# Paired token scores, output projections by seven products, fewer identity products at the start and a first refill in halves, in a one-core attention and mixture-of-experts block

## The chip, the cores and the metric

The kernel runs on one core of one Trainium2 chip. The metric is the device time of one execution in microseconds (us), the median of the runs that were made. All data are float32. The engines are PE (TensorE), DVE (VectorE), ACT (ScalarE), POOL (GpSimd) and SP (SyncE, which issues most of the DMAs).

## What is computed

A block of one layer on 256 tokens of width 1024, with 256 memory rows: a token mixer, cross attention and a mixture of experts, each added to the running `x`. In the mixer, `nsa_mixer` scores each query against compressed keys, selected keys and window keys; with 256 tokens every block of keys is selected and the window holds all of them, so the two token softmaxes (selected, window) run over all earlier tokens. Cut to what the change touches:

```
s = einsum(q, k) * DA**-0.5            # 8 heads of 64, masked to kpos <= t; k_slc and k_win
p = softmax(s)                         # per head; then o = p @ v, gated
merged = sigmoid(gate_a) * (y_a @ w_up_a) + sigmoid(gate_b) * (y_b @ w_up_b)
x = x + merged @ w_o_mix               # 256 x 1024 by 1024 x 1024  ("om")
...
x = x + o @ w_o                        # the same shape, after cross attention  ("ro")
...
y = sum over the 4 best of 32 experts: ((u + 1) * g * sigmoid(1.702 g)) @ w_down[e]
```

## The kernel before

**Order of work.** Each engine has one hand-written stream of instructions, and semaphores join them. PSUM has eight banks of 128 x 512; every group of products has a name, and `group_order` lists the groups in the order in which PE makes them. `placed_groups` gives group i the bank i modulo 8. `begin(name)` makes PE wait until the bank's former group is drained, `end(name, ...)` counts it filled, and `drain` counts it drained. Engines that wait for a group call `filled_of` or `drained_of`.

**Stages.** First x is turned, normalized and projected (q, keys, values, gates). Then comes a loop of nine steps h over the eight heads. In step h PE turns the probabilities of head h-1 (`ta`, `tb`), makes the token scores of head h (`sc{h}_0`, `sc{h}_1`, L1103) and "filler" groups of 16 products (gates, keys and values of cross attention), besides pieces of the second mixer. DVE masks the scores (L1734) and takes maxima (L1738), ACT exponentiates (L737) and scales (L746). Heads 2c and 2c+1 lie in rows 0 to 63 and 64 to 127 of chunk c of `qT`.

**Output projections.** `project_and_turn` (PE) and `residual_and_turned` (DVE) run twice, for "om" and for "ro". PE makes four groups of eight products with 512 columns, one for each token tile t and each half n of the output; DVE adds each group to `x_tok` (L1833). Between them PE turns the sums into the feature layout (L875, L1215) and DVE applies the gain (L1569).

**Weights.** `ring` has six slots of 2 MB, which 22 pieces use in turn (`PIECES`); `LAST_USE` names the group whose filling frees a slot. The 32 experts follow: six pieces of 2 MB each, `gu0` to `gu3` and `dn0`, `dn1`. Even experts use the ring; odd ones have five slots of their own (`r_odd`) made from buffers of the earlier stages, and share the ring's slot of `dn1`. SP issues the pieces in a fixed order and waits before each until its slot is free. Pieces of experts 0 and 1 are loaded during the earlier stages (`first_block`, `odd_half`, `odd_piece`); `even_heads(1)` then waits for expert 0 to free `gu0` and starts the refills.

**Experts.** `expert_block` takes 64 slots of tokens: `gate_up` reads gu0 to gu3 (L1331), then the former block's result is scattered (L1324), hidden rows are turned, and `down` reads dn0 and dn1. `gather_half` (L1308) fetches tokens.

**Start.** `keep_busy(o, n)` (L905) makes n products of the identity with itself into a bank that nobody reads. Here it is called with 5, 4, 3 and 8. A float32 product is two MATMUL rows in the trace; a turn is one.

```
            for n, t in ((0, 0), (0, 1), (1, 0)):
                residual(prefix, n, t, scale)
```

## Time and profile before

| | |
|---|---|
| median of three runs | 1299.54 us (1298.63 to 1300.12) |
| the profiled execution, its own time | 1298.83 us |
| span of its profile | 1297.1 us |
| mean granted TensorE clock | 0.991 |
| PE busy | 1244.9 us, 96% |
| DVE, ACT, POOL busy | 288.7 us, 145.3 us, 8.2 us |
| DMA | 454.70 MB, mean 351 GB/s |

The profile is of one execution. An engine's busy share is a mean over stages with different limits, so it has to be read by stage. A wait is put down to the engine, the tile and the line that ended it. In the trace the duration of a MATMUL row contains its fill and drain; consecutive rows overlap, so the time of many is read from the start of the first and of what follows, or from the chain of waits, which doesn't count an overlap twice.

### The profile page before, as it was taken

To read this page: it belongs to the slowest core of one execution; us is meant where nothing else is said; L and a number is where in the kernel's file an instruction comes from. 1 tells how busy PE (TensorE), PEld (TensorE's weight loads), DVE (VectorE), ACT (ScalarE), POOL (GpSimd) and SP (SyncE) were. 2 spreads that over 40 slices of the span, in tenths; PEclk is the share of its full clock that TensorE was granted. 3 is DMA by queue.
4 is the path that set the end of the run, shared out by engine and by line. 5 is a ranking of instruction groups with operands and counts; after the bars stand their busy time and mean duration, and the time that the engine had idled before them with its cause. 6 is when DMAs were issued, how large, how long until landed. Compare 5 with 4: busy or idle time off the path is not lost.

```text
span 1297.1 us, 14906 instructions
## 1 busy us (share of the span) xinstructions
PE 1244.9 (96%) x6197; PEld 614.1 (47%) x6197; DVE 288.7 (22%) x697; ACT 145.3 (11%) x325; POOL 8.2 (1%) x34
## 2 busy tenths in 40 slices
PE   9999999999999999999999999999989899999986
PEld 8868886757644343333343333443333344333322
DVE  2362234321132221111121111221111132211112
ACT  2223232101310000000000000000000000000001
POOL 1000000000000000000000000000000000000000
PEclk9999999999999999999999999999999999999998
DMA  9953233357559999999999999999999999999995
GB/s 332 318 194 110 85 131 113 115 195 268 203 195 401 428 428 427 426 427 428 429 429 428 428 429 429 427 428 428 428 428 428 428 428 427 427 427 428 427 425 238
DMA packets 60451, 454.70 MB, mean 351 GB/s; under 512 B 7228, under 2 KB 14072, under 8 KB 35064
## 3 DMA queue, kind: packets, MB, share of 16 engines
q1 hardware_dynamic: 58168, 452.49, 84.9%
q10 hardware_dynamic: 2240, 1.58, 0.4%
q8 instruction: 34, 0.56, 0.2%
q14 instruction: 9, 0.07, 0.0%
HBM read 453.00 MB, written 1.05 MB: 350 GB/s over the span
## 4 chain that ended last, share of the span: by engine, by line
PE 68%; DMA 29%; SPq 1%; issue 1%; DVE 1%; ACT 0%; POOL 0%; DVEq 0%; POOLq 0%; ACTq 0%
PE ps L1331 30%; DMA r_odd<-in_w_gu_dram 17%; PE ps L886 13%; DMA ring<-in_w_down_dram 11%; PE ps L893 7%; PE ps L1308 3%; PE ps L1324 3%; PE ps L1405 2%; PE ps L939 1%; PE ps L1103 1%; PE ps L1432 1%; SPq L494 1%; PE ps L1427 1%; PE ps L905 1%; PE ps L1252 1%
## 5 line engine op out<-in xcount | busy, mean ns | idle before, releaser
L1331 PE MATMUL ps<-r_odd,r_memT 128*64 128x512 f32 x1024 | 226.7, 597 | 15.3 <-DMA r_odd<-in_w_gu_dram 15.2
L1331 PE MATMUL ps<-ring,r_memT 128*64 128x512 f32 x1024 | 225.8, 594 | 11.9 <-DMA ring<-in_w_gu_dram 11.2
L1331 PE MATMUL ps<-ring,r_kx 128*64 128x512 f32 x768 | 176.9, 609 | 11.2 <-DMA ring<-in_w_down_dram 11.2
L1997 DVE TENSOR_SCALAR r_ga<-ps 128x512 f32<-128x512 f32 x32 | 22.1, 692 | 637.6 <-PE ps L1331 637.6
L1331 PEld LDWEIGHTS ps<-r_odd,r_memT 128*64 128x64 f32 x1024 | 73.4, 138 | 166.4 <-issue 137.2
L1331 PEld LDWEIGHTS ps<-ring,r_memT 128*64 128x64 f32 x1024 | 71.8, 137 | 160.2 <-issue 135.7
L886 PE MATMUL ps<-r_odd,ring 128*128 128x256 f32 x576 | 129.5, 383 | 0.0
L886 PEld LDWEIGHTS ps<-r_odd,ring 128*128 128x128 f32 x576 | 109.5, 192 | 18.0 <-issue 3.2
L1331 PEld LDWEIGHTS ps<-ring,r_kx 128*64 128x64 f32 x768 | 54.9, 140 | 130.0 <-issue 108.0
L827 ACT ACTIVATE r_ga<-r_ga 128x512 f32<-128x512 f32 x32 | 20.2, 630 | 462.8 <-DVE r_ga L1997 462.8
L1308 PE MATMUL ps<-r_dm,r_x 128*128 128x128 f32 x512 | 65.8, 282 | 0.0
L1324 PE MATMUL ps<-r_kx,r_dm 64*128 64x512 f32 x256 | 63.6, 615 | 0.7 <-ACT r_kx L833 0.7
L1308 PEld LDWEIGHTS ps<-r_dm,r_x 128*128 128x128 f32 x512 | 62.8, 197 | 1.6 <-DVE r_dm L1927 0.8
L1331 PE MATMUL ps<-r_gbx,r_kx 128*64 128x512 f32 x256 | 58.5, 598 | 0.8 <-DVE r_kx L2010 0.8
L833 ACT ACTIVATE r_kx<-ps 128x512 f32<-128x512 f32 x32 | 19.1, 597 | 333.9 <-PE ps L1331 333.9
L893 PE MATMUL ps<-ring,r_memT 128*128 128x512 f32 x112 | 49.2, 595 | 0.0
L1324 PEld LDWEIGHTS ps<-r_kx,r_dm 64*128 64x128 f32 x256 | 22.0, 186 | 41.3 <-issue 39.7
L1935 DVE TENSOR_TENSOR r_memT<-ps,sm 128x512 f32<-128x512 f32 x32 | 22.1, 692 | 64.6 <-PE ps L1308 64.6
L1331 PEld LDWEIGHTS ps<-r_gbx,r_kx 128*64 128x64 f32 x256 | 16.9, 136 | 40.6 <-issue 27.4
L1405 PE MATMUL ps<-r_ga,r_kx 32*64 32x512 f32 x256 | 35.8, 612 | 0.0
L893 PEld LDWEIGHTS ps<-ring,r_memT 128*128 128x128 f32 x112 | 21.0, 190 | 25.5 <-issue 25.2
L886 PE MATMUL ps<-r_memT,ring 128*128 128x256 f32 x128 | 28.6, 381 | 0.0
(342 smaller groups left out, 804.1 us busy)
## 6 DMA issues: line engine op xcount, KB each, us to landing
ring<-in_w_gu_dram SPq DMA_DIRECT2D x64, 2048.0 KB, 27.9
r_odd<-in_w_gu_dram SPq DMA_DIRECT2D x60, 2048.0 KB, 27.5
ring<-in_w_down_dram SPq DMA_DIRECT2D x47, 2048.0 KB, 22.6
r_gbx<-in_w_down_dram SPq DMA_DIRECT2D x15, 2048.0 KB, 30.2
ring<-in_w_in_dram SPq DMA_DIRECT2D x7, 2048.0 KB, 13.7
r_odd<-in_w_gu_dram SPq DMA_DIRECT2D x8, 1024.0 KB, 13.3
ring<-in_w_k_x_dram SPq DMA_DIRECT2D x2, 2048.0 KB, 9.5
ring<-in_w_v_x_dram SPq DMA_DIRECT2D x2, 2048.0 KB, 7.9
```

Source lines behind the costliest of these rows:

```text
L494: sp.dma_start(odd_slot[j], gu_dram[e, j] if j < 4 else dn_dram[e, j - 4]).then_inc(odd_loaded[j], 16)
L827: nc.scalar.activation(sig, gact, ACT.Sigmoid, scale=1.702).then_inc(sig_done, 1)
L833: nc.scalar.activation(y_slot, ps[:, ZBK, :], ACT.Copy).then_inc(yslot_ready, 1)
L886: last = mm(o[:, j * T:(j + 1) * T], w(k), src[:, k, :], start=(k == 0), stop=(k == kk - 1))
L893: last = mm(o, src[:, k, t * P:(t + 1) * P], w[:, k, 0:n], start=(k == 0), stop=(k == C - 1))
L905: mm(o[:, 0:P], ident[:], ident[:], start=True, stop=True)
L1308: last = mm(ps[:, buf, c * P:(c + 1) * P], x_rows[:, t, 2 * q + c // 2, c % 2], place[:, t], start=(t == 0), stop=(t == 1))
L1324: last = mm(ps[:, YB + 2 * t + n, :], scat[half, t * P:(t + 1) * P], y_slot[half, :], start=False, stop=False, skip_group_check=True)
L1331: last = mm(ps[n * SLOTS:(n + 1) * SLOTS, bk, :], stationary_, moving(n), start=start, stop=stop, skip_group_check=True)
L1405: mm(ps[n * SLOTS:(n + 1) * SLOTS, GBK + b, :], cur[q * NE:(q + 1) * NE, :], bgu_rows[q * NE:(q + 1) * NE, :], start=True, stop=False, ski ...
L1935: V.tensor_tensor(xg[:, buf, 4 * q:4 * q + 4], ps[:, bank_, :].rearrange("p (c s) -> p c s", c=4), gain_half[q], ALU.mult).then_inc(xg_rea ...
L1997: V.tensor_scalar(gact, ps[:, GBK, :], 7.0, None, ALU.min).then_inc(g_limited, 1)
```

## The change

- **Token scores.** For even h both heads h and h+1 are made in step h, their products alternating between rows 0 to 63 and rows 64 to 127. The odd head's two groups have banks 6 and 7 to themselves in this stage; all other groups of the stage share banks 0 to 5.
- **Output projections.** Each is cut into 2 x 2 blocks and made by seven products of blocks (P1 to P7, each four PE products with 512 columns) in place of eight. DVE makes four sums of blocks of the source (512 elements a row, in `sums`, the buffer `r_tp`) and four sums of blocks of the weights (2048 elements a row, in place in the ring), and adds every product to one to four quarters of `x_tok`: 14 additions in place of 4.
- **First refill.** Expert 2's `gu0` is loaded in two halves, the first as soon as expert 0 has used that half.
- **Order on SP.** Since `sums` lies in the buffer of an odd slot, `odd_half(1, 1, 0)` goes behind P5 of "ro", and `dn0` of expert 0 ahead of it.
- **Start.** `keep_busy` is called with 2, 1, 2 and 6.

```diff
+SEVEN = (1, 2, 3, 6, 7, 5, 4)
+ADDED_TO = {1: ((0, 1), (0, 0), (1, 0), (1, 1)), 2: ((0, 1),), 3: ((0, 0),), 6: ((0, 0), (1, 0), (1, 1)),
+            7: ((1, 0), (1, 1)), 5: ((0, 0), (1, 0)), 4: ((1, 1),)}
...
-            g += [f"sc{h}_0", f"sc{h}_1"] + filler_names(h)[:1]
+            if h % 2 == 0:
+                g += [f"sc{h + m}_{t}" for t in range(TT) for m in range(2)]
+            g += filler_names(h)[:1]
...
-    g += ["om0_0", "om0_1", "om1_0", "tx0", "tx1", "om1_1", "tx2", "tx3"]
+    g += [f"omP{n}" for n in SEVEN] + ["tx0", "tx1", "tx2", "tx3"]
...
+    first, last = order.index("sc0_0"), order.index("ub0")
+    pairs, turn = [], 0
+    for i, name in enumerate(order):
+        if first <= i < last and name[:2] == "sc" and int(name[2]) % 2:
+            pairs.append((name, BANKS - 2 + int(name[4])))
+            continue
+        n = BANKS - 2 if first <= i < last else BANKS
+        pairs.append((name, turn % n))
+        turn += 1
...
+        sums = r_tp.rearrange("p (s k t) -> p s k t", s=4, k=4)
...
+            first_block(range(4, 5))
+            filled_of(sp, "roP5")
             odd_half(1, 1, 0)
-            first_block(range(4, 6))
+            first_block(range(5, 6))
             sp.wait_ge(sq_done, 7)
             odd_half(1, 2, 1)
             filled_of(sp, "rt")
             odd_half(1, 1, 1)
 
-            even_heads(1)
+            s = eslot["gu0"]
+            rows2 = ring[:, s].rearrange("p (k n) -> p k n", k=2)
+            sp.wait_ge(first_half_freed, 1)
+            sp.dma_start(rows2[:, 0], gu_dram[2, 0][:, 0]).then_inc(first_half_loaded, 16)
+            sp.wait_ge(freed[s], 1)
+            sp.dma_start(rows2[:, 1], gu_dram[2, 0][:, 1]).then_inc(loaded[s], 16)
+            even_heads(1, range(1, HEADS))
...
-                        drained_of(act, f"{prefix}0_{t}")
-                        drained_of(act, f"{prefix}1_{t}")
+                        drained_of(act, f"{prefix}P{(5, 4)[t]}")
...
-            keep_busy(bank("q1"), 5)
+            keep_busy(bank("q1"), 2)
...
-            keep_busy(bank("q1"), 4)
+            keep_busy(bank("q1"), 1)
...
-            keep_busy(bank("q1"), 3)
+            keep_busy(bank("q1"), 2)
...
-            keep_busy(bank("q1"), 8)
+            keep_busy(bank("q1"), 6)
...
-                    for t in range(TT):
-                        o = begin(f"sc{h}_{t}")
-                        n = P * (t + 1)
-                        for b in range(2):
-                            last = mm(o[:, b * n:(b + 1) * n], qT[half * DA:(half + 1) * DA, c, t * P:(t + 1) * P],
-                                      kskw[half * DA:(half + 1) * DA, b, g, 0:n], start=True, stop=True)
-                        end(f"sc{h}_{t}", last)
+                    if h % 2 == 0:
+                        c, g = h // 2, h // PAIRS
+                        for t in range(TT):
+                            n = P * (t + 1)
+                            oo = [begin(f"sc{h + m}_{t}") for m in range(2)]
+                            for b in range(2):
+                                for m in range(2):
+                                    strip = slice(m * DA, (m + 1) * DA)
+                                    last = mm(oo[m][:, b * n:(b + 1) * n], qT[strip, c, t * P:(t + 1) * P],
+                                              kskw[strip, b, g, 0:n], start=True, stop=True)
+                                    if b == 1:
+                                        end(f"sc{h + m}_{t}", last)
...
+            def project_and_turn(prefix, piece_name, src, turned, ready, turn):
+
+                w1, w2 = wslot(f"{piece_name}1", C, 512), wslot(f"{piece_name}0", C, 512)
+
+                def product(n, lhs, rhs, part=range(4)):
+                    o = begin(f"{prefix}P{n}") if part[0] == 0 else bank(f"{prefix}P{n}")
+                    for k in part:
+                        last = mm(o, lhs(k), rhs[:, k], start=(k == 0), stop=(k == 3), skip_group_check=True)
+                    if part[-1] == 3:
+                        end(f"{prefix}P{n}", last)
+
+                def upper_left(k):
+                    ready(k)
+                    return src[:, k, 0:P]
+
+                def upper_right(k):
+                    ready(4 + k)
+                    return src[:, 4 + k, 0:P]
+
+                weights(f"{piece_name}1")
+                product(1, upper_left, w1[:, 0:4])
+                product(2, upper_right, w1[:, 4:8])
+                weights(f"{piece_name}0")
+                pe.wait_ge(sums_ready, 5 * turn + 1)
+                product(3, lambda k: sums[:, 3, k], w2[:, 4:8])
+                pe.wait_ge(sums_ready, 5 * turn + 3)
+                product(6, lambda k: sums[:, 1, k], w1[:, 0:4])
+                product(7, lambda k: sums[:, 2, k], w2[:, 0:4])
+                pe.wait_ge(sums_ready, 5 * turn + 4)
+                product(5, lambda k: sums[:, 0, k], w2[:, 4:8])
+                pe.wait_ge(sums_ready, 5 * turn + 5)
+                product(4, lambda k: src[:, 4 + k, P:2 * P], w1[:, 4:8], range(2))
+                drained_of(pe, f"{prefix}P5")
                 transpose4(f"{turned}0", x_tok, 0)
                 transpose4(f"{turned}1", x_tok, 1)
-                token_group(prefix, piece_name, src, 1, 1, ready)
+                product(4, lambda k: src[:, 4 + k, P:2 * P], w1[:, 4:8], range(2, 4))
                 oo = [begin(f"{turned}2"), begin(f"{turned}3")]
                 for t in range(TT):
-                    drained_of(pe, f"{prefix}1_{t}")
+                    drained_of(pe, f"{prefix}P{(2, 4)[t]}")
...
+                    if is_block(i, 2) and j == 0:
+                        pe.wait_ge(first_half_loaded, 16)
...
+                        if is_block(i, 0) and kk == 0:
+                            last.then_inc(first_half_freed, 1)
...
+            def residual_and_turned(prefix, piece_name, src, scale, turned, g0, turn):
+
+                w1, w2 = wslot(f"{piece_name}1", C, 512), wslot(f"{piece_name}0", C, 512)
+                b11, b21, b12, b22 = w1[:, 0:4], w1[:, 4:8], w2[:, 0:4], w2[:, 4:8]
+                a11, a12, a21, a22 = (src[:, k:k + 4, t:t + P] for t in (0, P) for k in (0, 4))
+
+                def product_added(n):
+                    name = f"{prefix}P{n}"
+                    filled_of(dve, name)
+                    for t, half in ADDED_TO[n]:
+                        xv = x_tok[:, t, half * 512:(half + 1) * 512]
+                        last = V.scalar_tensor_tensor(out=xv, in0=bank(name), scalar=scale, in1=xv, op0=ALU.mult, op1=ALU.add)
+                    drain(name, last)
+                    drained_of(dve, name)
+
+                link(V.tensor_tensor(sums[:, 0], a21, a22, ALU.add))
+                V.tensor_tensor(sums[:, 2], a11, a21, ALU.subtract)
+                link(V.tensor_tensor(sums[:, 1], sums[:, 0], a11, ALU.subtract))
+                V.tensor_tensor(sums[:, 3], a12, sums[:, 1], ALU.subtract).then_inc(sums_ready, 1)
+                for slot in (f"{piece_name}0", f"{piece_name}1"):
+                    dve.wait_ge(loaded[slot_of[slot]], need[slot])
+                V.tensor_tensor(b12, b22, b12, ALU.subtract).then_inc(sums_ready, 1)
+                dve.wait_ge(sums_ready, 5 * turn + 2)
+                filled_of(dve, f"{prefix}P1")
+                V.tensor_tensor(b11, b12, b11, ALU.add).then_inc(sums_ready, 1)
+                dve.wait_ge(sums_ready, 5 * turn + 3)
+                product_added(1)
+                product_added(2)
+                filled_of(dve, f"{prefix}P3")
+                V.tensor_tensor(b22, b22, b11, ALU.subtract).then_inc(sums_ready, 1)
+                product_added(3)
+                product_added(6)
+                V.tensor_tensor(b21, b21, b11, ALU.subtract).then_inc(sums_ready, 1)
+                product_added(7)
+                product_added(5)
                 gained(f"{turned}0", hT, g0, 0)
                 gained(f"{turned}1", hT, g0, 1)
-                residual(prefix, 1, 1, scale)
+                product_added(4)
                 gained(f"{turned}2", hT, g0, 2)
                 gained(f"{turned}3", hT, g0, 3)
 
             dve.wait_ge(x_again, 16)
-            residual_and_turned("om", 0.5, "tx", R_X)
+            dve.wait_ge(merged_ready, 4)
+            residual_and_turned("om", "om", sga, 0.5, "tx", R_X, 0)
...
+            drained_of(dve, "ox3")
+            residual_and_turned("ro", "ox", oxT, 1.0, "tf", R_FFN, 1)
```

**How the order moves.** PE, the score stage from step 0 to step 1 (L1103 before, L1134 after: token scores; L886/L914 fillers; L1086 to L1093 and L1114 to L1121: turns). Before:

```order
L1103 MATMUL ps<-r_odd,r_gbx 128x128 x2
L1103 MATMUL ps<-r_odd,r_gbx 128x256 x2
L886 MATMUL ps<-r_odd,ring 128x256 x32
L1086 MATMUL ps<-ident,r_odd 128x128 x4
L1090 MATMUL ps<-ident,r_odd 128x128 x2
L1093 MATMUL ps<-ident,r_odd 15x128 x2
L1103 MATMUL ps<-r_odd,r_gbx 128x128 x2
L1103 MATMUL ps<-r_odd,r_gbx 128x256 x2
L886 MATMUL ps<-r_odd,ring 128x256 x16
```

After:

```order
L1134 MATMUL ps<-r_odd,r_gbx 128x128 x4
L1134 MATMUL ps<-r_odd,r_gbx 128x256 x4
L914 MATMUL ps<-r_odd,ring 128x256 x32
L1114 MATMUL ps<-ident,r_odd 128x128 x4
L1118 MATMUL ps<-ident,r_odd 128x128 x2
L1121 MATMUL ps<-ident,r_odd 15x128 x2
L914 MATMUL ps<-r_odd,ring 128x256 x16
```

The scores of head 1 now stand with those of head 0, ahead of step 0's fillers; the same repeats for heads 3, 5 and 7.

DVE, the projection "om" (L1833/L1897: additions to x; L1569/L1626: gain; L1901 to L1904: sums of the source; L1907 to L1918: sums of the weights). Before:

```order
L1833 SCALAR_TENSOR_TENSOR r_x<-ps,r_x 128x512 x3
L1569 TENSOR_TENSOR r_odd<-ps,vT 128x512 x2
L1833 SCALAR_TENSOR_TENSOR r_x<-ps,r_x 128x512
L1569 TENSOR_TENSOR r_odd<-ps,vT 128x512 x2
```

After:

```order
L1904 TENSOR_TENSOR r_odd<-r_ga,r_odd 128x512
L1907 TENSOR_TENSOR ring<-ring 128x2048
L1910 TENSOR_TENSOR ring<-ring 128x2048
L1897 SCALAR_TENSOR_TENSOR r_x<-ps,r_x 128x512 x5
L1915 TENSOR_TENSOR ring<-ring 128x2048
L1897 SCALAR_TENSOR_TENSOR r_x<-ps,r_x 128x512 x4
L1918 TENSOR_TENSOR ring<-ring 128x2048
L1897 SCALAR_TENSOR_TENSOR r_x<-ps,r_x 128x512 x4
L1626 TENSOR_TENSOR r_odd<-ps,vT 128x512 x2
L1897 SCALAR_TENSOR_TENSOR r_x<-ps,r_x 128x512
L1626 TENSOR_TENSOR r_odd<-ps,vT 128x512 x2
```

Four long operations and ten more additions stand between PE's groups, in an order that PE's products wait for.

SP, the queue of weight loads from the projection "ro" to the first refills (L483/L504: ring; L491/L512: halves of odd slots). Before:

```order
L491 DMA r_odd<-in_w_gu_dram 128x2048 [waits filled5]
L491 DMA r_odd<-in_w_gu_dram 128x2048
L483 DMA ring<-in_w_down_dram 128x4096 [waits filled7]
L483 DMA ring<-in_w_down_dram 128x4096 [waits filled3]
L491 DMA r_odd<-in_w_gu_dram 128x2048 [waits sq_done]
L491 DMA r_odd<-in_w_gu_dram 128x2048 [waits filled5]
L483 DMA ring<-in_w_gu_dram 128x4096 [waits freed4]
L483 DMA ring<-in_w_gu_dram 128x4096 [waits freed5]
```

After:

```order
L512 DMA r_odd<-in_w_gu_dram 128x2048 [waits filled0]
L504 DMA ring<-in_w_down_dram 128x4096 [waits filled6]
L512 DMA r_odd<-in_w_gu_dram 128x2048 [waits filled6]
L504 DMA ring<-in_w_down_dram 128x4096 [waits filled7]
L512 DMA r_odd<-in_w_gu_dram 128x2048 [waits sq_done]
L512 DMA r_odd<-in_w_gu_dram 128x2048 [waits filled5]
L561 DMA ring<-in_w_gu_dram 128x2048 [waits first_half_freed]
L563 DMA ring<-in_w_gu_dram 128x2048 [waits freed4]
L504 DMA ring<-in_w_gu_dram 128x4096 [waits freed5]
```

A load of 1 MB moves behind P5 of "ro", and the first refill is two loads with a wait each.

## Rows read from the trace of the kernel before

**Rows 1.** The page's slices, 40 equal ones over the span

```profile
DMA  9953233357559999999999999999999999999995
GB/s 332 318 194 110 85 131 113 115 195 268 203 195 401 428 428 427 426 427 428 429 429 428 428 429 429 427 428 428 428 428 428 428 428 427 427 427 428 427 425 238
```

**Rows 2.** Stretches: us, PE busy (count), other engines where given, PEclk, DMA share, GB/s

```profile
100.00:385.00 285.00, 283.42 (x1245) 1.00 0.44 161
...
384.00:386.00 2.00, 2.00 (x10) 0.58 (x12) 0.69 (x1) 0.00 (x0) 0.00 (x0) 1.00 0.00 0
386.00:388.00 2.00, 2.00 (x12) 0.57 (x8) 0.00 (x0) 0.00 (x0) 0.00 (x0) 1.00 0.00 0
```

**Rows 3.** Timeline of SP's queue: the first two refills, start and us

```profile
388.61 0.33 SPq L483 DMA_DIRECT2D ring<-in_w_gu_dram  x1
394.27 0.33 SPq L483 DMA_DIRECT2D ring<-in_w_gu_dram  x1
```

**Rows 4.** Stretches of half a microsecond after the second refill's issue

```profile
395.00:395.50 0.50, 0.50 (x6) 0.21 (x4) 0.00 (x0) 0.00 (x0) 0.00 (x0) 1.00 0.85 262
...
396.00:396.50 0.50, 0.50 (x4) 0.14 (x2) 0.00 (x0) 0.00 (x0) 0.00 (x0) 1.00 0.70 197
```

**Rows 5.** Timeline of PE, 0 to 12 us: start, us, line, operation

```profile
2.15 2.50 PE L905 MATMUL ps<-ident 128*128 128x128 f32 x10 [2.15 <-POOL ident L599]
...
6.65 2.63 PE L918 MATMUL ps<-ident,r_x 128*128 128x128 f32 x16
...
9.79 0.61 PE L926 MATMUL ps<-ident,sm 128*128 128x128 f32 x4
10.24 1.95 PE L905 MATMUL ps<-ident 128*128 128x128 f32 x16
12.02 13.98 PE L939 MATMUL ps<-r_odd,ring 128*128 128x256 f32 x64
```

**Rows 6.** Timelines of ACT and of DVE, 0 to 15 us

```profile
4.12 1.06 ACT L679 ACTIVATE r_odd<-r_x 128x1024 f32<-128x1024 f32 x1 [1.20 <-DMA r_x<-in_x_dram]
...
5.46 1.23 DVE L1577 SCALAR_TENSOR_TENSOR r_odd<-r_x 128x1024 f32<-128x1024 f32 x1 [5.46 <-DMA r_x<-in_x_dram]
...
7.24 0.17 DVE L1585 RECIPROCAL sm<-sm 128x2 f32<-128x2 f32 x1 [0.27 <-ACT sm L681]
10.93 3.23 DVE L1591 SCALAR_TENSOR_TENSOR r_odd<-ps,vT,r_dm 128x256 f32<-128x256 f32 x8 [3.52 <-ACT r_dm L669]
```

**Rows 7.** DMA issues, 0 to 30 us: the halves of the query weights, us to landing

```profile
ring<-in_w_in_dram SPq DMA_DIRECT2D x2, 1024.0 KB, 7.7
```

**Rows 8.** Chain that ended last: start, us, what; small products and scores

```profile
83.73 1.89 PE ps L1040 x32
85.62 1.67 PE ps L1103 x8
...
103.55 1.50 PE ps L1103 x8
...
425.94 1.92 PE ps L1324 x8
```

**Rows 9.** Chain that ended last: the projection "om"

```profile
269.33 20.60 PE ps L893 x48
289.93 0.87 PE ps L875 x8
290.80 6.88 PE ps L893 x16
```

**Rows 10.** Timeline of PE and of ACT at the last head's turn

```profile
234.13 0.60 PE L1086 MATMUL ps<-ident,r_odd 128*128 128x128 f32 x4
...
231.89 1.49 ACT L746 ACTIVATE r_odd<-r_odd,sm 128x128 f32<-128x128 f32 x4 [5.52 <-DVE sm L1745]
```

**Rows 11.** Timeline of DVE around "om"

```profile
270.09 0.69 DVE L1826 TENSOR_TENSOR r_ga<-r_ga,r_gbx 128x512 f32<-128x512 f32 x1
...
289.96 0.69 DVE L1833 SCALAR_TENSOR_TENSOR r_x<-ps,r_x 128x512 f32<-128x512 f32 x1 [6.17 <-PE ps L893]
290.57 1.28 DVE L1569 TENSOR_TENSOR r_odd<-ps,vT 128x512 f32<-128x512 f32 x2
```

**Rows 12.** Groups of DVE with 1024 elements: busy us, mean ns

```profile
L1795 DVE TENSOR_TENSOR r_odd<-r_odd 128x1024 f32<-128x1024 f32 x1 | 1.2, 1225 | 0.0
```

**Rows 13.** Stretches of 1 us of PE, at the first token scores

```profile
86.00:87.00 1.00, 1.00 (x6) 0.81 1.06 410
...
88.00:89.00 1.00, 1.00 (x4) 0.50 0.14 41
89.00:90.00 1.00, 1.00 (x4) 0.50 0.00 0
```

36 lines of the change are left out of this document (9 added, 27 removed).

## The prediction

> **What bounds the kernel now.** I read the slices first. The row GB/s stands at 425 to 429 from the fourteenth slice (about 420 us) to the last but one: from there the expert weights stream without a gap [rows 1]. Ahead of that the stretches show the reverse: PE is busy 283.42 of 285 us between 100 and 385 us, at full clock and with DMA at 0.44, and from 384 to 388 us nothing moves at all [rows 2]. SP issues the first refill at 388.61, when PE has used `gu0` of expert 0 [rows 3]. So the kernel has two parts: PE sets when the stream of refills starts, and the stream (30 experts of 6 pieces of 2.10 MB, 377 MB, at 428 GB/s 882 us) sets the rest, with a tail after its last byte. A microsecond taken from PE's path ahead of 388.6 should come off the end whole, as long as DMA still waits for PE there. A microsecond taken from PE later is worth nothing. The chain of waits says the same: PE lines up to 388, then PE and DMA in turn.
>
> **Start.** Nine of twenty identity products go. In the trace a product is two instructions: ten take 2.50 us, 0.50 a product, and the last sixteen 1.95 us, 0.24 a product [rows 5]. So PE starts at 1.2 GHz and reaches 2.4 in between, though the clock column says 1.00 there. They stand on the path only where nothing else is late. The first half of x is there at about 4.1 and the second at 5.4 [rows 6], but the turns start at 6.65 [rows 5]. After: two products end at 3.2, one at 3.7, the turns run from 4.2 to 6.8 at the same 2.63 us; two products at 0.24 to 0.50 end at 7.3 to 7.8; the row of roots needs DVE's reciprocal, which ends at 7.41 [rows 6]; its 0.61 us end at about 8.4. Then the path over ACT and DVE to the first turned chunk takes what it does now: from PE's end at 10.40 to DVE's start at 10.93, and two of eight DVE operations (0.8 us) [rows 5, 6]. That gives 9.75; six products give 9.8. The first weights land at 1.69 + 7.7 = 9.4 [rows 7] (1.69 is their issue; the 7.7 is the median of both halves). So the projection starts near 10.3 in place of 12.02: **1.7 us**. Bounds: 0.3, if PE is still at 1.2 GHz there (roots end at 8.7, six products of 0.50 at 11.7), and 2.4, if only the landing holds it.
>
> **Token scores.** Eight heads take 1.67 + 7 x 1.50 = 12.2 us [rows 8]. What a pair takes when its halves alternate the trace doesn't show for this shape. The nearest row is the scatter, which alternates the same two row halves and two banks: eight instructions of 512 columns in 1.92 us [rows 8], where full-height ones take 20.60/48 = 0.43 each [rows 9], 3.43 us in sequence. So halves do run side by side: 1.72 us for the half, and 0.20 beside it. A head's columns at that rate are 4 x 0.107 + 4 x 0.214 = 1.28 us; a pair side by side is the same 1.28, plus the present overhead of 0.22: 1.50. Small instructions alternating halves cost 1.89/32 = 0.059 us each with their weight load [rows 8], 0.94 for a pair's sixteen, so weight loads don't bind, but in the 128-column part (eight, 0.47 against 0.43) they just do. I take 1.55 a pair, 6.2 in all: **6.0 us** less. Ends: 1.5 (6.2 less), and 3.0, nothing gained.
>
> The Trainium skill (TensorE: Matmul & The Clock Gate, LDWEIGHTS) gives a weight load as its columns by 1.2 GHz, 107 ns for 128. If a pair's sixteen loads came one after another at that, a pair would take 1.9 us and the term would be 4.5. The row of 32 small instructions disagrees for halves that alternate: 59 ns.
>
> Does something else become late? Odd steps lose 1.5 us of PE between `tb` and the filler, but the odd head's scores are then there already, and its softmax starts when it does now. The tightest place is the last head: ACT's scaling ends at 233.38 and PE's turn begins at 234.13, slack 0.75 [rows 10]; both hang on the filler before, so both move together. With six banks in place of eight, every group of the stage takes a bank whose former user was drained microseconds before (the fillers are 7 us long). I cost both at nothing; their cover is these fillers.
>
> **Output projections.** PE makes 28 products in place of 32. One is 20.60/24 = 0.858 us [rows 9], so each projection can lose 3.43 us, if DVE keeps up. DVE's times: 0.61 from one 512-element operation to the next, 0.73 when the next waits for it [rows 11]; 1.225 for 1024 elements [rows 12], so each further 512 cost 0.535, and the 2048 of a weight sum, which the trace lacks, about 2.30. From PE's start of P1: the last merge ends at +1.5; four source sums +4.3 (P3 needs them at +6.9); first weight sum +6.6, second +8.9 (P6 needs it at +10.3); P1's four additions and P2's one +12.3; third weight sum, after P3, +14.6 (P5 at +17.2); additions of P3 and P6 +17.3; fourth weight sum +19.6 (P4 at +20.6); additions of P7 and P5 +22.3. PE has made half of P4 at +22.3 and waits for P5's additions, about 0.15. Then turns (0.87 [rows 9]), the other half at +25.0, and the tail as now. Slacks of 1.4, 2.6 and 1.0 us hide the rest. "ro" is the same with DVE 0.7 us earlier. Together 2 x (3.43 - 0.15) = **6.6 us**. If a weight sum took 3 us instead of 2.3, the four would put P4 1.8 us late, each time: 3.0 in all.
>
> **Loads on SP.** `gu0` of expert 0 goes after P5 of "om" (+20.6) instead of the second group (+13.7), `gu1` after P4 (+25.0 for +27.8); expert 0 is 90 us away. In "ro", from P5 on, 3.1 MB, then 2.1, then twice 1.05 MB are to be loaded: 7.3 MB at 428 GB/s, 17.2 us, from about 363 to 381 on the clock of before less what is gained ahead of "ro". The first half of the refill is asked for at 386.8 - 3.3 = 383.5 on that clock. Two microseconds of idle DMA remain, so the order costs nothing; without that cover the stream would start late.
>
> **First refill in halves.** The first MB starts 1.8 us earlier (half of `gate_up`'s 3.6 us on `gu0`). But the second refill waits for `gu1`, 5.66 us after the first [rows 3], and 2.1 MB take 4.9 us: the queue is nearly empty there already, 262 and 197 GB/s [rows 4]. What is gained runs into that gap. I take **0.2 us**, between -0.2 (one more start) and 0.9 (the lost bandwidth of that gap).
>
> **Sum.** 1.7 + 6.0 + 6.6 + 0.2 = 14.5 us. The profiled execution took 1298.83, so 1284.3; the median of the runs is 0.7 above it: **1285.0 us**.
>
> **Rivals.**
> 1. *PE stays at 1.2 GHz longer at the start.* By 0.3 for 1.7 the sum is 13.1: 1286.4. For: ten cold instructions at 0.25 us. Against: PE had long come to full speed at 10.24. The Trainium skill (same page, the HAM clock gate) makes the low clock the default that activity lifts; that rule speaks against taking products out here.
> 2. *Halves don't run side by side for products this short.* Then 8.5 is left: 1291.0. Against: the scatter row. A bound by weight loads in part lies between.
> 3. *DMA is late.* If the reordered loads need 2 us more than the idle time, or the refills after `gu1` catch up with less, 3 to 6 us of the gain go: about 1289.
> 4. *DVE becomes the bound of the projections, slower than before.* The four weight sums are in its chain: with p for one of them the fourth is there at +10.4 + 4p (the +19.6 above), and PE needs it at +20.6. The whole gain and 2.6 us more are gone when 2 x (4p - 10.2) = 17.1, at p = 4.7 us for 2048 elements, twice the rate of [rows 12]: 1302. For: the operation works in place on slots that PE reads at that time. Against: no DVE row in the trace is slowed by PE.
>
> A drift on top: PE falls to 1.2 GHz from 86.8 to 90, after the small products [rows 13], which costs 1.6 us. Paired scores change what comes before; the fall may vanish, or another appear: 1.5 us either way.
>
> **How the numbers follow.** Forecast 0.74, rival 1 0.10, rival 2 0.05, rival 3 0.07, rival 4 0.02; 0.02 for no change. Best ends of all terms (0.7, 0.2, 0.3, 0.7) and the clock's 1.5 give 1281.6. Upwards, rival 1, the scores at 4.5 and 1.5 us of clock give 1289.4. I take 1282 to 1290. Faster by over 0.2% (2.6 us, about what a measurement of this kernel can tell) 0.96, same 0.02, slower 0.02.
>
> **What would show it.** Right: the first refill's halves issued near 372.5 and 374.3; 1.5 to 1.6 us for a pair's scores; each projection near 26.4 us from P1 to the next stage's start, before 29.8; 2048-element sums at 2.3 us; GB/s at 428 as early as the refills. Wrong: waits of PE on DVE's sums or on a drained bank, a projection after 11.5 us at the start, or idle DMA after the refills begin.

## The result and the profile after

| | before | after |
|---|---|---|
| median of the runs compared | 1299.41 us (1298.63 to 1300.12, 4 runs) | 1280.92 us (1279.55 to 1282.43, 4 runs) |
| ratio of the times, 95% interval | | 0.9864 [0.9843, 0.9886] |
| the profiled execution, own time / span | 1298.83 / 1297.1 us | 1279.55 / 1277.8 us |
| mean granted TensorE clock | 0.991 | 0.995 |
| PE busy, DVE busy | 1244.9, 288.7 us | 1227.0, 324.3 us |

The change made the kernel faster by 18.5 us in these medians. The prediction said 14.5; its forecast of 1285.0 is 4.1 us too high, and the time lies 1.1 us below the range of 1282 to 1290. The ratio is the recorded one; the two medians alone give 0.9858.

The slices of the page after, as in [rows 1]: the stream is whole from the thirteenth slice and not the fourteenth (a slice is 31.9 us).

```profile
DMA  9953233257489999999999999999999999999996
GB/s 333 310 214 132 83 116 132 99 202 278 169 341 429 425 430 428 426 428 427 430 429 428 428 427 431 429 428 427 427 430 430 428 426 427 428 428 427 427 428 270
```

SP's queue after (start, us), to be set against [rows 3]:

```profile
370.35 0.33 SPq L561 DMA_DIRECT2D ring<-in_w_gu_dram  x1
372.07 0.33 SPq L563 DMA_DIRECT2D ring<-in_w_gu_dram  x1
377.74 7.19 SPq L504 DMA_DIRECT2D ring<-in_w_gu_dram  x3
```

The second half goes where the whole refill went before: 372.07 for 388.61, **16.54 us earlier**. `gu1` follows 5.67 us later, as before, and the early first half runs into the same gap, as these stretches after show (last column GB/s):

```profile
373.00:375.00 2.00, 2.00 (x16) 1.31 (x16) 0.85 (x2) 0.00 (x0) 0.00 (x0) 1.00 0.98 360
...
377.00:379.00 2.00, 2.00 (x12) 0.72 (x10) 0.00 (x0) 0.00 (x0) 0.00 (x0) 1.00 0.79 188
379.00:381.00 2.00, 2.00 (x12) 0.61 (x10) 0.00 (x0) 0.00 (x0) 0.00 (x0) 1.00 0.62 221
```

PE's start after, against [rows 5]. The turns (L946) take 3.67 us and not 2.63, 0.23 us each where they take 0.12 in the profiles of only_scores and only_products: PE runs them at 1.2 GHz, though the clock column says 1.00 here. Yet the projection (L967) starts at 10.66 in place of 12.02, 1.36 us earlier.

```profile
4.41 3.67 PE L946 MATMUL ps<-ident,r_x 128*128 128x128 f32 x16
7.88 0.79 PE L933 MATMUL ps<-ident 128*128 128x128 f32 x4
8.51 0.61 PE L954 MATMUL ps<-ident,sm 128*128 128x128 f32 x4
8.95 1.50 PE L933 MATMUL ps<-ident 128*128 128x128 f32 x12
10.66 3.69 PE L967 MATMUL ps<-r_odd,ring 128*128 128x256 f32 x16 [0.20 <-DVE r_odd L1648]
```

The token scores after (L1134; timeline of PE, start and us):

```profile
100.24 0.38 PE L1121 MATMUL ps<-ident,r_odd 128*15 128x128 f32 x2
100.45 7.07 PE L914 MATMUL ps<-r_odd,ring 128*128 128x256 f32 x32
...
120.48 1.58 PE L1134 MATMUL ps<-r_odd,r_gbx 64*128 64x128 f32 x16
121.99 7.17 PE L914 MATMUL ps<-r_odd,ring 128*128 128x256 f32 x32
```

A pair takes 121.99 - 120.48 = 1.51 us. The first two rows are the odd step 1: the filler now follows the turns by 0.21 us. The same place before:

```profile
103.17 0.38 PE L1093 MATMUL ps<-ident,r_odd 128*15 128x128 f32 x2
103.48 1.57 PE L1103 MATMUL ps<-r_odd,r_gbx 64*128 64x128 f32 x8
104.98 7.17 PE L886 MATMUL ps<-r_odd,ring 128*128 128x256 f32 x32
```

From the last turn to the filler there were 1.81 us with the scores' 1.50 inside; now 0.21, and the filler is 0.10 shorter in its row. So an odd step takes about 0.2 us less, beside the scores themselves. The fall of the clock in [rows 13] is gone in this execution:

```profile
86.00:90.00 4.00, 4.00 (x20) 3.54 (x19) 3.43 (x11) 0.55 (x3) 0.00 (x0) 1.00 0.18 62
```

The projection "om" after, PE and then DVE (timeline):

```profile
259.45 7.03 PE L1234 MATMUL ps<-ring,r_ga 128*128 128x512 f32 x16
266.32 13.90 PE L1234 MATMUL ps<-ring,r_odd 128*128 128x512 f32 x32
280.05 1.88 PE L1234 MATMUL ps<-ring,r_ga 128*128 128x512 f32 x4
281.77 1.04 PE L903 MATMUL ps<-ident,r_x 128*128 128x128 f32 x8
...
285.88 6.50 PE L914 MATMUL ps<-r_odd,ring 128*128 128x256 f32 x29
```

```profile
263.83 2.29 DVE L1907 TENSOR_TENSOR ring<-ring 128x2048 f32<-128x2048 f32 x1
266.15 2.29 DVE L1910 TENSOR_TENSOR ring<-ring 128x2048 f32<-128x2048 f32 x1
...
276.57 2.29 DVE L1918 TENSOR_TENSOR ring<-ring 128x2048 f32<-128x2048 f32 x1
```

From P1 to the next stage these are 26.43 us, where before took 29.83 (269.16 to 298.99); in "ro" 26.35 for 29.79. The weight sums take 2.29 us, and the fourth ends at 278.86, 1.2 us before P4 starts at 280.05. The second ends at 268.44, 1.3 us before P6 is due. In these two projections PE waits for none of the sums, and P5's additions end at 281.61, just ahead of the turns at 281.77.

At the end, SP's writes of the result, before and then after (timeline):

```profile
1290.53 3.80 SPq L585 DMA_DIRECT2D out_dram<-r_x  x4
```

```profile
1273.17 2.51 SPq L614 DMA_DIRECT2D out_dram<-r_x  x4
```

The code of the four writes is the same in both kernels, but here they were issued over 2.51 us in place of 3.80, and landed in 2.0 in place of 3.2 (median). From DVE's last operation to the end of the span there were 4.43 us before and are 2.48 now: 1.95 us that no term of the prediction has.

### The profile page after: what moved, and what is told of

Same layout as the page of the kernel before. It is cut to its first block, busy times and chain, and to the rows that moved or that the text cites. A ratio compares the mean times of both kernels' runs of the same rounds, so it can differ in the third digit from the quotient of the medians.

```text
span 1277.8 us, 14901 instructions
## 1 busy us (share of the span) xinstructions
PE 1227.0 (96%) x6163; PEld 603.2 (47%) x6163; DVE 324.3 (25%) x733; ACT 145.2 (11%) x325; POOL 8.1 (1%) x34
## 4 chain that ended last, share of the span: by engine, by line
PE 70%; DMA 28%; SPq 1%; DVE 1%; issue 1%; ACT 0%; DVEq 0%; ACTq 0%
PE ps L1384 32%; DMA r_odd<-in_w_gu_dram 16%; PE ps L914 13%; DMA ring<-in_w_down_dram 12%; PE ps L1234 4%; PE ps L921 3%; PE ps L1361 3%; PE ps L1377 3%; PE ps L1458 2%; PE ps L967 1%; PE ps L1489 1%; PE ps L1484 1%; PE ps L1305 1%; PE ps L1287 1%; SPq L515 1%
## 5 line engine op out<-in xcount | busy, mean ns | idle before, releaser
L914 PE MATMUL ps<-r_odd,ring 128*128 128x256 f32 x576 | 128.0, 380 | 0.0
L914 PEld LDWEIGHTS ps<-r_odd,ring 128*128 128x128 f32 x576 | 108.5, 190 | 16.8 <-issue 2.3
L914 PE MATMUL ps<-r_memT,ring 128*128 128x256 f32 x128 | 28.5, 381 | 0.0
L1234 PE MATMUL ps<-ring,r_odd 128*128 128x512 f32 x64 | 27.8, 592 | 0.0
L914 PEld LDWEIGHTS ps<-r_memT,ring 128*128 128x128 f32 x128 | 24.0, 190 | 3.8 <-issue 0.7
## 6 DMA issues: line engine op xcount, KB each, us to landing
r_odd<-in_w_gu_dram SPq DMA_DIRECT2D x8, 1024.0 KB, 14.5
```

The source lines that it names most:

```text
L914: last = mm(o[:, j * T:(j + 1) * T], w(k), src[:, k, :], start=(k == 0), stop=(k == kk - 1))
L1234: last = mm(o, lhs(k), rhs[:, k], start=(k == 0), stop=(k == 3), skip_group_check=True)
```

## The experiments

**How they are read.** Single executions of one kernel scatter by 1 to 7 us (before: 1294.8 to 1300.1 in 42 runs), which is more than most effects here. So every profile is cut at two marks: q, the start of the query projection, and R, SP's issue of the second half (or the whole) of expert 2's `gu0`. "q to R" is PE's path, in "rest" the expert weights stream to the end of the span.

| kernel | median us (runs) | ratio [interval] | q | q to R | rest |
|---|---|---|---|---|---|
| before | 1299.41 (4) | | 12.02 | 376.59 | 908.49 |
| only_scores | 1290.81 (4) | 0.9949 [0.9930, 0.9967] | 10.83 | 368.16 | 908.21 |
| only_products | 1290.06 (4) | 0.9934 [0.9914, 0.9954] | 11.24 | 371.38 | 905.98 |
| only_start | 1296.31 (12) | 0.9989 [0.9977, 1.0002] | 10.46 | 375.02 | 906.32 |
| only_halves | 1298.51 (12) | 1.0008 [0.9998, 1.0019] | 12.19 | 376.58 | 907.53 |
| after | 1280.92 (4) | 0.9864 [0.9843, 0.9886] | 10.66 | 361.41 | 905.73 |
| heads_in_turn | 1280.05 (4) | 0.9864 [0.9845, 0.9884] | 9.94 | 363.45 | 906.11 |
| dve_more | 1284.26 (4) | 0.9905 [0.9884, 0.9927] | 10.94 | 364.29 | 905.87 |
| three_halves | 1280.33 (4) | 0.9865 [0.9845, 0.9886] | 11.23 | 361.38 | 907.29 |
| start_less | 1279.31 (4) | 0.9866 [0.9845, 0.9887] | 9.94 | 361.38 | 905.68 |
| same_half | 1289.67 (5) | 0.9936 [0.9916, 0.9957] | 10.15 | 368.26 | 906.29 |
| heads_apart | 1284.04 (4) | 0.9891 [0.9873, 0.9909] | 11.17 | 363.60 | 908.03 |
| after_again | 1280.78 (4) | 0.9865 [0.9845, 0.9886] | 10.78 | 361.42 | 907.90 |
| start_less_again | 1280.43 (4) | 0.9867 [0.9848, 0.9886] | 10.43 | 361.38 | 905.79 |

Ratios are to the runs of before that were made with them; those have medians of 1298.33 us for the four only_ kernels, 1297.94 for heads_in_turn, dve_more, three_halves and start_less, and 1298.72 for same_half, heads_apart, after_again and start_less_again. Kernels that run the same program from q to R agree there to 0.04 us, so long as the clock does the same.

**only_scores**: the kernel before with the pairs and their banks alone.

```diff
+            if h % 2 == 0:
+                g += [f"sc{h + m}_{t}" for t in range(TT) for m in range(2)]
```

> The kernel before with the paired token scores alone. Theory 1 (everything comes from PE's path ahead of the first refill): 1.5 us for a pair's scores in place of 3.0, and 0.2 us more for each place where scores no longer stand between turns and fillers: 6.9 us; 8.4 us if the fall of the clock at 86 to 90 us is gone as well, and then block 0 and the end both come that much earlier. Theory 2 (the unforeseen part of the gain lies in the stream or at the end): 6.0 us before block 0 and more at the end. On the clock: if the paired scores themselves prevent the fall, it is gone here; if it was the shift in time, it may be back.

Its profile has no clock fall at the scores. Neither has only_start's, and that one has the scores of before; so 375.02 - 368.16 = **6.86 us** is what the pairs take away, 0.9 more than the 6.0 predicted, and Theory 1's 6.9.

**only_products**: before with `SEVEN` products, DVE's sums and the order on SP alone.

```diff
-    g += ["om0_0", "om0_1", "om1_0", "tx0", "tx1", "om1_1", "tx2", "tx3"]
+    g += [f"omP{n}" for n in SEVEN] + ["tx0", "tx1", "tx2", "tx3"]
```

> The kernel before with the seven products alone. Theory 1: 3.4 us from each projection, 6.8 in all, block 0 and the end earlier by as much; the clock falls at 86 us as before, since nothing ahead of it changed. Rival (DVE's chain is close to binding): under 6 us, with waits of PE on the sums of more than 0.2 us each.

Here the clock fall came, and longer, from 85 to 91.6 us, and the first head's scores took 2.53 us, as the next two rows show:

```profile
84.68 2.60 PE L1112 MATMUL ps<-r_odd,r_gbx 64*128 64x128 f32 x8
87.21 10.96 PE L895 MATMUL ps<-r_odd,ring 128*128 128x256 f32 x39
```

So its 371.38 holds some 3 us of low clock and can't be read straight. "om" runs from 270.05 to 296.45, 26.40 us, as after. From the profiles of only_scores and after, which have no fall, the products are 368.16 - 361.41 = **6.75 us**, for 6.6 predicted. (These two differ in the start too, but that lies ahead of q.)

**only_start**: before with `keep_busy` of 2, 1, 2 and 6.

```diff
-            keep_busy(bank("q1"), 5)
+            keep_busy(bank("q1"), 2)
```

> The kernel before with fewer identity products at the start alone. Theory 1: the first projection starts 1.4 us earlier (10.7 for 12.0), block 0 as well, and the whole is 1.3 to 1.4 us faster. If the fall of the clock at 86 us depends on when the small products come and not on what they are, it may be gone here, and the gain is 2.8. Rival: the clock rises later and the gain is under 0.5 us.

With the products at the start as before, q came at 12.02, 12.19, 10.83 and 11.24; with fewer at 10.66, 10.46, 9.94, 10.94, 11.23, 10.15, 11.17 and 10.78. The means are 11.57 and 10.67, so the start gives **0.9 us**, with a scatter as large. The whole time can't show it: the interval of the ratio reaches from 0.9977 to 1.0002. q to R is 1.57 us below that of before: that is the clock fall of [rows 13], which did not come here, with the scores unchanged.

**only_halves**: before with the first refill in halves.

```diff
+            sp.wait_ge(first_half_freed, 1)
+            sp.dma_start(rows2[:, 0], gu_dram[2, 0][:, 0]).then_inc(first_half_loaded, 16)
```

> The kernel before with the first refill in halves alone. Theory 1: block 0 starts where it did (384.9 us), the first half is on its way 1.7 us earlier, but the second refill waits for PE as before and the stream after it is the same: 0.0 us, within 0.3. Theory 2 (the halves carry a part of what came unforeseen): 1.5 to 2 us faster.

The times are the same within the interval, R lies where it did (388.77 for 388.61), and q to R is 376.58 for 376.59. **0 us.**

**three_halves**: the changed kernel with `gu0`, `gu1` and `gu2` of expert 2 in halves.

```diff
+            for j in range(3):
+                s = eslot[f"gu{j}"]
...
+                sp.wait_ge(first_half_freed, j + 1)
```

> The changed kernel with expert 2's gu0, gu1 and gu2 all refilled in halves, each half asked for when expert 0 has used it. Theory A (one piece in halves gains nothing, since its early megabyte runs into the idle gap ahead of the second piece): with gu1 and gu2 in halves too, the queue never runs dry: DMA moves more than 350 GB/s between 376 and 381 us where it moved 98 and 33 in two half microseconds, and the steady stream is 1.4 to 1.9 us earlier at expert 1's end and at every refill from there; the time is 1.4 to 1.9 us shorter, about 1279.2. The rival (the further starts and waits cost as much, or PE's use of the pieces and not the stream sets the pace there) says: within 0.3 us of the changed kernel.

The rival was right, for a reason of its own. The first fence is the changed kernel, the second three_halves (stretches; GB/s last); each pair stands at the same distance from R.

```profile
377.02:380.02 3.00, 3.00 (x16) 1.01 (x14) 0.00 (x0) 0.00 (x0) 0.00 (x0) 1.00 0.67 161
393.35:395.35 2.00, 2.00 (x12) 0.72 (x10) 0.00 (x0) 0.00 (x0) 0.00 (x0) 1.00 0.96 377
```

```profile
377.56:380.56 3.00, 3.00 (x16) 1.01 (x14) 0.00 (x0) 0.00 (x0) 0.00 (x0) 1.00 1.00 369
393.90:395.90 2.00, 2.00 (x12) 0.71 (x10) 0.00 (x0) 0.00 (x0) 0.00 (x0) 1.00 0.88 287
```

The gap is filled, and a smaller one comes back 16 us later. Added up over stretches of 1 us from the first half's issue, the changed kernel has moved 6.82 MB after 20 us and 10.95 after 30; three_halves 7.18 and 10.85. Up to there SP asks for a piece when PE has freed it, so what is loaded by then is set by PE's pace: the first piece of `down` is asked for at 392.81 in three_halves and at 392.28 in the changed kernel, 20.20 and 20.21 us after R. That fits one piece in halves giving nothing. The time, 1280.33, is that of the changed kernel within its scatter, and not the 1279.2 expected.

**heads_in_turn**: in each tile the two products of one head (four instructions; where the expectations say products, they count instructions) ahead of those of the other.

```diff
-                            for b in range(2):
-                                for m in range(2):
+                            for m in range(2):
+                                for b in range(2):
```

> The changed kernel with the same pairs, banks and order of groups, but the four products of the even head's rows of an output tile before those of the odd head, instead of alternating. Theory A (row halves run side by side only when neighbouring products lie in different halves): in every tile only the products at the border of the two heads overlap, a pair takes 2.8 to 3.1 us instead of 1.5 to 1.6, and the first refill is issued 5 to 6 us later than in the changed kernel's profile (370.35, so 375.4 to 376.4); the time is about 1286 us. The rival (the gain of the pairs comes from fewer changes between kinds of products and from fewer waits, not from alternation) says: 1.5 to 1.9 us a pair, first refill within 1 us of 370.35. The 0.2 us for each of the four odd steps that no longer have scores between turns and fillers should stay: fillers follow the turns by 0.2 us and take 7.07 us, as in the changed kernel.

Theory A fell: the median is 1280.05 us and not 1286. A pair takes 123.12 - 121.50 = 1.62 us, 0.11 more than alternating, so q to R should be 0.44 longer; the other 1.6 us are a clock fall from 84 to 88 us.

```profile
121.50 1.68 PE L1134 MATMUL ps<-r_odd,r_gbx 64*128 64x128 f32 x16
123.12 7.17 PE L914 MATMUL ps<-r_odd,ring 128*128 128x256 f32 x32
```

That left open whether row halves matter at all, hence the next two.

**same_half**: both heads' scores from rows 0 to 63, so the odd heads' own scores are left out.

```diff
-                                    strip = slice(m * DA, (m + 1) * DA)
+                                    strip = slice(0, DA)
```

> The changed kernel, with the odd head's scores made from the even head's rows too (rows 0 to 63 for both, so the odd heads' own scores are left out); number, order, banks and shapes of the products are unchanged. With the heads one after the other a pair still took 1.62 us in place of 1.51, so alternation is not what the gain needs. Theory A (two row halves run side by side even over runs of four products): on one half the sixteen products follow one another, a pair takes 2.7 to 2.8 us (1.28 us more for the second head's columns), the first refill is issued 4.5 to 5 us later relative to the start of the query projection than in the changed kernel (359.7 us after it) and the time is about 1285.5. The rival (a short group's cost is a fixed price for the change of kind, and sixteen short products cost hardly more than eight on any rows) says 1.5 to 1.7 us a pair and no difference in time.

```profile
122.91 2.88 PE L1134 MATMUL ps<-r_odd,r_gbx 64*128 64x128 f32 x16
125.73 7.17 PE L914 MATMUL ps<-r_odd,ring 128*128 128x256 f32 x32
```

2.82 us a pair: the rival is out, and side by side is shown. The second head costs 1.31 us on the same rows and nothing on the others (1.51 against the 1.50 of one head before). Four times 1.31 is 5.2; the other 1.6 of the 6.85 us in q to R are a clock fall again, from 85.9 to 89.1 us. The median, 1289.67, is 4 us above the 1285.5 expected, and the five runs lie between 1286.54 and 1292.56; the profile is of the fastest, and what the slower ones lost beyond this is open.

**heads_apart**: all eight instructions of one head, then the eight of the other.

```diff
+                        for m in range(2):
+                            for t in range(TT):
...
+                                for b in range(2):
```

> The changed kernel with all eight products of the even head ahead of all eight of the odd head, in the same four banks. If halves run side by side only while the sequencer can look a few products ahead, runs of eight overlap in part: a pair takes 1.9 to 2.6 us, the first refill 1.6 to 4.4 us later relative to the query projection than the changed kernel's 359.7 us. If each half has a queue of its own that holds eight products, a pair still takes 1.5 to 1.7 us. If the price is that of the change of kind alone (the rival of the run before), also 1.5 to 1.7, but then the run on one half shows it too.

```profile
159.02 2.13 PE L1134 MATMUL ps<-r_odd,r_gbx 64*128 64x128 f32 x16
161.07 4.15 PE L914 MATMUL ps<-r_memT,ring 128*128 128x256 f32 x18
```

2.05 us a pair, and q to R is 2.19 longer, four times 0.55. This is the expectation's first case, 1.9 to 2.6. So the overlap shrinks with the length of a run on one half: 1.51, 1.62 and 2.05 us for runs of two, four and eight instructions. On one half, with no overlap, it is 2.82.

**dve_more**: one source sum made three more times in each projection.

```diff
+                for _ in range(3):
+                    link(V.tensor_tensor(sums[:, 2], a11, a21, ALU.subtract))
```

> The changed kernel with one source sum of 512 elements made three times more, each waiting for the one before, so some 2.2 us more in DVE's chain of each projection, with the same result. By the slack terms of the prediction (1.4 us at P3, 2.6 us at P6, 1.0 to 1.2 us at P4) the sums for P4 come 1.0 to 1.2 us late: PE's wait ahead of P4 grows to about 1 us in om and to 0.3 to 1.2 us in ro, the refills start 1.3 to 2.4 us later (371.7 to 372.8 against 370.35) and the time is about 1.3 to 2.4 us longer. If DVE is the bound already (rival 4 in a mild form: its chain sets the end with no slack), it is 4.4 us longer in all. If DVE has more slack than worked out, nothing changes and PE still waits 0.35 us for P5's additions.

```profile
270.96 10.57 PE L1234 MATMUL ps<-ring,r_odd 128*128 128x512 f32 x24 [0.77 <-DVE ring L1912]
281.38 1.98 PE L1234 MATMUL ps<-ring,r_ga 128*128 128x512 f32 x4
283.90 1.09 PE L903 MATMUL ps<-ident,r_x 128*128 128x128 f32 x8 [0.54 <-DVE r_x L1897]
```

2.14 us more on DVE made "om" 1.87 us longer and "ro" 1.02, q to R 2.88. In "om" PE waits first at P6 (slack 1.4 in the prediction, 0.77 late here), in both again for P5's additions, which stand behind the fourth sum: the expectation had the wait ahead of P4 only. So "om" hid 0.27 of the 2.14 us and "ro", where DVE begins earlier, 1.12: the slack is about a microsecond or less, and most of any further work on DVE comes off the gain. Both 2.88 and the median of 1284.26 us, 3.3 above the changed kernel's, are more than the 1.3 to 2.4 expected.

**start_less** and **start_less_again**: the changed kernel without the two identity products ahead of the row of roots.

```diff
-            keep_busy(bank("q1"), 2)
```

> The changed kernel without the two identity products ahead of the row of roots. Theory A (these two stand beside DVE's reciprocal, and what is behind them waits for that): the query projection starts within 0.2 us of the changed kernel's 10.66, and the time is the same within 0.3 us. The rival (PE's clock rises later when products are taken out here): the identity products from 8 us on take 0.25 us each instead of 0.12 and the projection starts 0.5 to 1.5 us later, or parts of it run at 1.2 GHz, so that the scores start 0.5 us or more later than 84.17.

```profile
4.25 3.67 PE L946 MATMUL ps<-ident,r_x 128*128 128x128 f32 x16
7.72 0.67 PE L953 MATMUL ps<-ident,sm 128*128 128x128 f32 x4
8.23 1.50 PE L933 MATMUL ps<-ident 128*128 128x128 f32 x12
9.94 4.34 PE L966 MATMUL ps<-r_odd,ring 128*128 128x256 f32 x19 [0.20 <-DVE r_odd L1647]
```

> The changed kernel without the two identity products ahead of the row of roots, timed beside the changed kernel. By the first look they stood on the path where the clock was still low (0.79 us for four instructions): the query projection starts at 9.94 in place of 10.66 where the clock rises late, and at the same time where it rises early. So 0.3 to 0.7 us shorter than the changed kernel in the median, less than the spread of single runs. If the products are what raises the clock, some executions show a projection that begins at 1.2 GHz and the median is 0.5 us or more longer.

q came at 9.94 and 10.43, where the changed kernel had 10.66 and 10.78, all four with turns of 3.67 or 3.68 us. So the two products did stand on the path there, and Theory A, within 0.2 us of 10.66, missed as well. The medians, 1279.31 and 1280.43, stand against 1280.92 and 1280.78: lower both times, but by less than its runs scatter (1278.79 to 1281.38), so a gain isn't shown. A later rise of the clock, the rival, was not seen in either profile.

**after_again**: the changed kernel once more.

> The changed kernel unaltered, a second look and five rounds. The spread of its four runs (1279.6 and 1282.3, nothing between) should come from two things that differ from one execution to the next and not with the kernel: when PE's clock rises at the start (before or after the turns of x, about 0.7 us), and how long the last writes take after DVE's last operation (2.5 us in six of the profiles so far, 3.9 to 4.5 in three). Median 1280 to 1282. If the pairs keep the clock up, there is no clock fall between 83 and 92 us; if its absence was chance, one may appear (1.5 us).

Both clusters came again (1279.67, 1279.73; 1281.82, 1282.16). The expected causes of them were only half of it. The last writes were short this time (2.50 us); the time went in expert 31 instead. The chain that ended last shows it. In the first profile of the changed kernel (first fence) it waits for the last weights, and PE then has eight instructions left; in after_again (second fence) it waits for the piece ahead of them, and PE then has 32, in 8.60 us:

```profile
1215.36 40.44 DMA r_odd<-in_w_gu_dram
...
1255.84 1.94 PE ps L1384 x8
```

```profile
1214.20 37.21 DMA r_odd<-in_w_gu_dram
1251.46 8.60 PE ps L1384 x32
```

Thirty-two of this shape take 7.04 where the clock is full. PE runs the first of them at the low clock, 1.2 GHz, as these stretches show (PE busy is the second number, PEclk the third from the end):

```profile
1250.50:1252.50 2.00, 1.04 (x4) 0.43 (x6) 0.00 (x0) 0.00 (x0) 0.00 (x0) 0.66 1.02 426
1252.48:1254.48 2.00, 2.00 (x8) 0.59 (x6) 0.00 (x0) 0.00 (x0) 0.00 (x0) 0.50 1.00 414
```

The profiles of before and of heads_apart show such a fall of 3 to 4 us too, three_halves one at 1224 to 1228 us; the other ten show none in the last 45 us ahead of the last scatter. The rest after R lies between 905.7 and 906.3 us in eight of the fourteen profiles and between 907.3 and 908.5 in six, and each of the six has one of two things that the eight have not: 3.9 to 4.5 us behind DVE's last operation in place of 2.4 to 2.6 (before, only_scores, only_halves), or this late fall (before, heads_apart, after_again, three_halves). Earlier in the stream a fall costs nothing that can be seen: every profile has two or three between 550 and 720 us, at a granted clock of 0.50, and in the eight the rest agrees to 0.6 us all the same.

## Why the prediction was wrong

The direction and the mechanism of every term held, and the four terms together came out near their sum; the time fell below the range through two things that the sum leaves out: the fall of the clock, kept apart as "1.5 us either way", and the stretch behind the first refill, put at nothing. This is the account. The spans differ by 1297.1 - 1277.8 = 19.3 us:

| part | predicted | found in the two profiles |
|---|---|---|
| start | 1.7 | 1.36 (0.9 by the means over all profiles) |
| token scores | 6.0 | 6.86 |
| output projections | 6.6 | 6.75 |
| first refill in halves | 0.2 | 0.0 |
| clock fall at the scores | "may vanish", not in the sum | 1.57 |
| from R to the end | 0 | 2.76 |

The terms of the sum came out 0.5 us above the prediction (14.97 for 14.5), the last two rows 4.3 us.

- **Start.** The term was oversized, on the step "the turns run from 4.2 to 6.8 at the same 2.63 us". They took 3.67, by their length at the low clock for most of them. The roots ended at 9.1 and not at 8.4, and the path over DVE from there took 1.54 us for the forecast's 1.35: 9.75 becomes 10.66. The forecast stood only 0.4 off because it took 10.3 where its own working gave 9.75 to 9.8, for no reason given, and that was luck. (The best end is also off: with the landing at 9.4 alone the term would be 2.6 and not 2.4.) Rival 1 named the mechanism and was right in part: with fewer products ahead, PE reaches 2.4 GHz no sooner, so turns that come earlier run at 1.2.
- **Token scores.** 1.55 a pair forecast, 1.51 measured; shown to rest on the row halves by same_half. The price by weight loads of 107 ns each (the Trainium skill, TensorE: Matmul & The Clock Gate, LDWEIGHTS), one after another, 1.9 us a pair, does not hold here: sixteen loads and their instructions take 1.51 us together, 94 ns each, while the trace gives a load of these 187 ns, so loads overlap. What the term missed is 0.9 us: in four odd steps the turns are now followed by the filler directly, one change between kinds of products where there were two. The rows give about 0.2 us a step, and it stayed in every variant with pairs, alternating or not. The Trainium skill (TensorEngine Tiling (Array Packing), Key Properties) says that switching the tile mode drains the array; it gives no time. That this is what the 0.2 us are is not shown.
- **Output projections.** 26.43 and 26.35 us, for "near 26.4"; sums of 2.29 for 2.30; the slack at P4 is 1.2 for 1.0. The wait of 0.15 for P5's additions did not come, so each lost the whole 3.4 us. Rival 4 was far, as said, yet dve_more shows that its slope is real.
- **Halves.** Nothing in place of 0.2: the point "what is gained runs into that gap" was the whole truth. Rival 2 did not come, nor rival 3: the reordered loads had left the queue nearly idle from about 369.1 us, 1.3 us ahead of the first half's issue at 370.35, where the prediction had 2.
- **What failed, first:** the clock. The prediction knew the fall of the clock at 86.8 us, priced it at 1.6 and left it out of the sum as "1.5 us either way". The two profiles differ by 1.57 us there.
- **What failed, second:** the step "a microsecond taken from PE later is worth nothing", with the tail taken as fixed; the sum has no term behind R. It was 2.76 us shorter: 1.95 behind DVE's last operation, where the writes are, and 0.81 ahead of it, where before has its late fall. That PE can matter there after all is shown by after_again: the last weights are waited for, and a slow PE behind them costs time to the end.
- **The starting point.** The prediction measured itself against 1299.54, three runs that all lie in the upper of two clusters: the 42 runs of before have a mean of 1297.6, 15 of them at 1294.8 to 1296.1 and the others at 1297.9 to 1300.1. The eight runs of the changed kernel, half and half at 1279.6 to 1279.7 and 1281.8 to 1282.4, have a mean of 1280.9. Mean against mean the gain is 16.7 us (lower clusters 15.8, upper ones 16.7), of which the parts found here, with 0.9 for the start, are 14.5 and the fall up to 1.6; some 0.6 us is not accounted for. That the sum of the four terms is the predicted 14.5 again is luck, errors that cancel (0.9 and 0.1 too little, 0.8 and 0.2 too much).
- **The range.** Its lower end came from adding the best ends and the clock, 1281.6, rounded inward to 1282. No term stood for the end of the span, which varied by 2.8 us in the profiles.

**Left open: what the change does to the clock and to the writes.** None of the seven profiles with alternating pairs has a fall between 83 and 92 us; of the seven without alternation five do (before, only_products, only_halves, heads_in_turn, same_half) and two don't (only_start, heads_apart). That looks like more than chance, and would make the 1.57 us part of the change's gain; but the falls come and go for reasons not known here. Some comparisons change the scores alone (before with only_scores; heads_in_turn, same_half and heads_apart with after), but each side of them is one or two executions. The same holds for the writes: they were long in three of the five profiles built on before and in none of the nine built on the changed kernel. only_products and only_start, whose end is that of before, had the short ones. Whether the 1.95 us belong to the change or to the execution is therefore not shown.

## What to carry to other kernels

Before a forecast of a few microseconds, ask what the same kernel varies by and at which places; an execution's clock falls and last writes can be as large as a term, and a median of three runs can lie in one cluster. Give the end of the span a term or a width of its own. Cut profiles at marks that the change doesn't move, and compare stage by stage: there differences of 0.1 us can be read where whole times scatter by 3 and more. Asking for a transfer earlier brings nothing while the pieces behind it are paced by their consumer; the gap only moves.

## What the runs showed of the hardware

- Two products on different row halves overlap even when they don't alternate: 1.51 us for sixteen instructions on alternate halves, 1.62 in runs of four, 2.05 in runs of eight, 2.82 on one half. I had expected 2.8 to 3.1 for runs of four.
- PE at the start: after fewer warm-up products the turns of x took 3.67 us in eight of ten profiles with such a start, 3.44 and 2.71 in the other two; with the full number 2.63, 2.79, 1.91 and 1.91. So the moment at which the clock rises, read from the length of the rows, differs from one execution to the next.
- The clock can fall behind a wait: in expert 31 PE waited for weights and then ran some 3.5 us at a granted clock of 0.50 in three of fourteen profiles (waits of 2.34, 2.50 and 2.56 us). Four others had waits as long (2.45, 2.46, 2.61 and 2.62 us) and no fall.
- Four writes of 256 KB at the end were issued over 2.5 us and landed in 2.0 or 2.1 in eleven profiles; in before, only_scores and only_halves over 3.8, 3.9 and 3.3 us, landing in 3.2, 3.3 and 3.0.
